# The norms' factors spread by two f32r passes instead of one f32 product

## The reference

```
for l in range(2):                                   # model A; B has the same frame
    x = x + 0.5 * swiglu(rmsnorm(x, ffn1_norm[l]), w_ffn1_in[l], w_ffn1_out[l])
    u = rmsnorm(x, mix_norm[l])
    c_q, c_kv, k_r, hq, hf, hi, hgate, mq, gates = split(u @ w_in[l])
    q = rmsnorm(c_q, q_lat_norm[l]) @ w_uq[l]         # the latents' norms, in A alone
    ckv = rmsnorm(c_kv, kv_lat_norm[l])
    mem_n = rmsnorm(mem, mem_norm[l])                 # the memory's norm, in A alone
    ...
    x = x + merged @ w_out[l]
    x = x + 0.5 * swiglu(rmsnorm(x, ffn2_norm[l]), w_ffn2_in[l], w_ffn2_out[l])
return rmsnorm(x, final_norm)

rmsnorm(x, g) = x * rsqrt(mean(x * x, over the width) + 1e-6) * g
```

## Time and profile before

| | us |
|---|---|
| median of 3 runs | 2376.81 |
| lowest and highest | 2376.17, 2376.86 |
| the profiled execution | 2377.26 |
| its span, from the first instruction to the last | 2375.5 |
| PE busy (99%) | 2356.3 |
| DVE busy (69%) | 1648.9 |
| ACT busy (53%) | 1253.1 |
| POOL busy (15%) | 363.4 |

### The profile page before, as it was taken

How to read it: one execution, slowest core, us unless ns; L and a number is a source line. 1 busy time by engine, 2 the same in 40 slices (tenths; PEclk the granted TensorE clock), 3 DMA queues, 4 the chain that set the end, 5 groups by cost and what they waited for, 6 DMA issues and landing times.

```text
span 2375.5 us, 50987 instructions
## 1 busy us (share of the span) xinstructions
PE 2356.3 (99%) x21836; PEld 2296.3 (97%) x21836; DVE 1648.9 (69%) x2292; ACT 1253.1 (53%) x1788; POOL 363.4 (15%) x313
## 2 busy tenths in 40 slices
PE   9999999999999999999999999999999999999998
PEld 8999999999999999999999999989999999989998
DVE  7775787966667657878666766776665766776764
ACT  6554656654445456565454454645554454645553
POOL 4012020300200210203003003431002002431001
PEclk9999999999999999999999999999999999999999
DMA  7555433455555544345555655413555555412553
GB/s 258 188 195 187 169 127 141 178 195 190 187 191 193 199 178 177 109 143 181 199 191 178 227 186 193 163 69 108 197 194 179 197 184 193 169 71 101 203 196 124
DMA packets 57680, 410.21 MB, mean 173 GB/s; under 512 B 6384, under 2 KB 6640, under 8 KB 8688
## 3 DMA queue, kind: packets, MB, share of 16 engines
q1 hardware_dynamic: 56592, 402.15, 47.2%
q10 hardware_dynamic: 864, 4.82, 0.5%
HBM read 405.89 MB, written 1.05 MB: 171 GB/s over the span
## 4 chain that ended last, share of the span: by engine, by line
PE 92%; DVE 4%; issue 2%; ACT 2%; DMA 0%; POOL 0%; SPq 0%; DVEq 0%; POOLq 0%; ACTq 0%
PE bank L301 91%; DVE area L314 1%; DVE sb_wlo L314 1%; ACT area L310 1%; PE bank L305 1%; DMA sb_raw<-stream 0%; ACT sb_whi L310 0%; POOL sb_x_ssq L314 0%; DVE area L325 0%; DVE area L342 0%; SPq L395 0%; DVE area L352 0%; DVE sb_x L325 0%; DVE area L320 0%; DVE sb_x L314 0%
## 5 line engine op out<-in xcount | busy, mean ns | idle before, releaser
L301 PE MATMUL bank<-area,sb_whi 128*128 128x256 f32 x11752 | 2040.3, 279 | 4.0 <-ACT area L310 2.5
L301 PEld LDWEIGHTS bank<-area,sb_whi 128*128 128x128 f32 x11752 | 1780.4, 188 | 15.3 <-ACT area L310 5.2
L301 PE MATMUL bank<-area,sb_wlo 128*128 128x256 f32 x5876 | 1619.6, 278 | 2.4 <-DVE sb_wlo L314 2.4
L310 ACT ACTIVATE sb_whi<-sb_raw 128x1024 fp32r<-128x1024 f32 x762 | 800.1, 1057 | 730.5 <-PE bank L301 726.9
L301 PEld LDWEIGHTS bank<-area,sb_wlo 128*128 128x128 f32 x5876 | 1100.3, 188 | 4.0 <-DVE sb_wlo L314 3.8
L314 DVE TENSOR_TENSOR sb_wlo<-sb_raw,sb_whi 128x1024 fp32r<-128x1024 f32 x762 | 957.6, 1265 | 167.4 <-ACT sb_whi L310 166.1
L314 DVE TENSOR_TENSOR area<-area,area 128x256 f32<-128x256 f32 (+6 forms) x504 | 258.9, 523 | 233.2 <-ACT area L310 231.5
L310 ACT ACTIVATE area<-area 128x256 fp32r<-128x256 f32 (+5 forms) x487 | 230.5, 482 | 66.2 <-DVE area L314 55.6
L314 DVE TENSOR_TENSOR area<-bank,sb_x_diag 128x512 f32<-128x512 f32 x244 | 166.8, 684 | 32.8 <-PE bank L301 19.3
L301 PE MATMUL bank<-area,area 64*64 64x64 f32 (+5 forms) x2864 | 151.0, 250 | 0.2
L301 PEld LDWEIGHTS bank<-area,area 64*64 64x64 f32 (+3 forms) x2864 | 128.7, 139 | 19.4 <-issue 4.9
(11 more groups left out here) (82 smaller groups left out, 722.9 us busy)
## 6 DMA issues: line engine op xcount, KB each, us to landing
sb_raw<-stream SPq DMA_DIRECT2D x379, 1024.0 KB, 4.8
sb_raw<-stream SPq DMA_DIRECT2D x4, 512.0 KB, 7.5
area<-lora ACTq DMA_DIRECT2D x2, 768.0 KB, 4.6
area<-c ACTq DMA_DIRECT2D x1, 1504.0 KB, 8.5
sb_x<-x SPq DMA_DIRECT2D x4, 256.0 KB, 5.4
area<-mem ACTq DMA_DIRECT2D x1, 1024.0 KB, 6.8
out<-sb_x SPq DMA_DIRECT2D x4, 256.0 KB, 2.9
area<-m ACTq DMA_DIRECT2D x1, 512.0 KB, 3.6
```

The lines of the kernel that those rows point to most:

```text
L301: return lambda e: e.matmul(out, lhsT, rhs, start=start, stop=stop, skip_group_check=True, tile_position=at)
L310: return lambda e: e.activation(out, a, f, **kw)
```

## The change

The diagonal tile is made twice: `high`, rounded to f32r as it is written, and `low`, the product again less `high`. `spread_parts` multiplies both by a matrix of ones in f32r and adds the results in PSUM. This replaces the float32 product in `norm_spread` (norms of x, of the memory, and both at the boundary) and in `latents_norm`. The final norm keeps the float32 product (`parts=False`). The ones in f32r are made once, by a copy on ACT in `constants_ready`, for which PE waits. The new tiles lie in memory of their own; `sc.diag` stays as the place of `sc.rs`.

```diff
@@ -698,11 +698,34 @@
     if at is None:
         sc.ssq, sc.diag, sc.sq = (sbuf(k, f"{name}_{n}", [128, T])[:, :] for n in ("ssq", "diag", "sq"))
         sc.ms, sc.tm = (sbuf(k, f"{name}_{n}", [128, 2])[:, :] for n in ("ms", "tm"))
+        sc.parts = [sbuf(k, f"{name}_{n}", [128, T], F32R)[:, :] for n in ("high", "low")]
     else:
         sc.ssq, sc.diag, sc.sq = (area(k, at + T * i, T) for i in range(3))
         sc.ms, sc.tm = area(k, at + 3 * T, 2), area(k, at + 3 * T + 8, 2)
+        sc.parts = [area(k, at + (4 + i) * T, T, dt=F32R) for i in range(2)]
     sc.rs = sc.diag
     return sc
+
+
+def diagonal_parts(k, parts, tm):
+    dve, ident = k.dve, const(k, "ident")
+    high, low = parts
+    for i in range(tm.shape[1]):
+        c, scale = slice(128 * i, 128 * i + 128), tm[:, i:i + 1]
+        n = dve.mark(tensor_scalar(high[:, c], ident, scale, ALU.mult))
+        dve.wait(dve, n)
+        n = dve.mark(scalar_tensor_tensor(low[:, c], ident, scale, high[:, c].bitcast(F32), ALU.mult, ALU.subtract))
+    return n
+
+
+def spread_parts(k, out, parts):
+
+    for i, part in enumerate(parts):
+        n = k.pe.mark(matmul(out, k.ones_r, part, start=i == 0, stop=i == 1))
+    return n
 
 
 def square(k, sc, j, x):
@@ -724,7 +747,7 @@
     return n
 
 
-def norm_sums(k, sc, b, more=None):
+def norm_sums(k, sc, b, more=None, parts=True):
 
 
     pe, dve, pool = k.pe, k.dve, k.pool
@@ -742,6 +765,9 @@
     pool.wait(dve, n)
     sc.tm_done = pool.mark(tensor_tensor(sc.tm, sc.ms, col(k, COL_HALFNEG).to_broadcast([128, 2]), ALU.pow))
     dve.wait(pool, sc.tm_done)
+    if parts:
+        sc.diag_done = diagonal_parts(k, sc.parts, sc.tm)
+        return
     for i in range(2):
         sc.diag_done = dve.mark(tensor_scalar(sc.diag[:, 128 * i:128 * i + 128], const(k, "ident"),
                                               sc.tm[:, i:i + 1], ALU.mult))
@@ -750,7 +776,7 @@
 def norm_spread(k, sc, b):
 
     k.pe.wait(k.dve, sc.diag_done)
-    n = k.pe.mark(matmul(b[:, T:2 * T], const(k, "ones"), sc.diag))
+    n = spread_parts(k, b[:, T:2 * T], sc.parts)
     k.act.wait(k.pe, n)
     sc.rs_done = k.act.mark(activation(sc.rs, b[:, T:2 * T], ACT.Copy))
 
@@ -833,7 +859,7 @@
 def final(k):
 
     pe, dve, b = k.pe, k.dve, k.bank[3]
-    norm_sums(k, k.sx, b, k.last.more)
+    norm_sums(k, k.sx, b, k.last.more, False)
     pe.wait(dve, k.sx.diag_done)
     n = pe.mark(matmul(b[:, T:2 * T], const(k, "ones"), k.sx.diag))
     dve.wait(k.act, k.x_done[NX - 1])
@@ -890,10 +916,9 @@
     pool.wait(dve, n)
     n = pool.mark(tensor_tensor(f.tm, f.ms, col(k, COL_HALFNEG).to_broadcast([128, 4]), ALU.pow))
     dve.wait(pool, n)
-    ident = const(k, "ident")
-    for diag, c in ((k.sx.diag, 2), (f.diag, 0)):
-        for i in range(2):
-            n = dve.mark(tensor_scalar(diag[:, 128 * i:128 * i + 128], ident, f.tm[:, c + i:c + i + 1], ALU.mult))
+    f.parts = [area(k, SPARE + (5 + i) * T, T, dt=F32R) for i in range(2)]
+    for parts, c in ((k.sx.parts, 2), (f.parts, 0)):
+        n = diagonal_parts(k, parts, f.tm[:, c:c + 2])
     k.sx.diag_done = f.diag_done = n
 
 
@@ -1218,7 +1243,8 @@
 
     m.lat, m.lsq = area(k, 0, 6, T), area(k, 6 * T, 5, T)
     m.lat_hi, m.lat_lo = area(k, 11 * T, 5, T, dt=F32R), area(k, 16 * T, 5, T, dt=F32R)
-    m.lat_diag = m.lat_rs = area(k, 21 * T, 512)
+    m.lat_rs = area(k, 21 * T, 512)
+    m.lat_parts = [area(k, at * T, 512, dt=F32R) for at in (21, 25)]
     m.k_rot = [area(k, (23 + i) * T, T) for i in range(2)]
     m.q_rot = [area(k, 6 * T + 512 * i, 2, T) for i in range(2)]
     m.gates = [area(k, T * i if i < 20 else 44 * T + T * (i - 20), 2, T) for i in range(0, 24, 2)]
@@ -1337,16 +1363,14 @@
     pool.wait(dve, n)
     n = pool.mark(tensor_tensor(m.lat_tm, m.lat_ms, col(k, COL_HALFNEG).to_broadcast([128, 4]), ALU.pow))
     dve.wait(pool, n)
-    for i in range(4):
-        m.lat_diag_done = dve.mark(tensor_scalar(m.lat_diag[:, 128 * i:128 * i + 128], const(k, "ident"),
-                                                 m.lat_tm[:, i:i + 1], ALU.mult))
+    m.lat_diag_done = diagonal_parts(k, m.lat_parts, m.lat_tm)
 
 
 def latents_norm(k, m, l):
     pe, act, dve = k.pe, k.act, k.dve
     b = k.bank[6]
     pe.wait(dve, m.lat_diag_done)
-    n = pe.mark(matmul(b[:, :], const(k, "ones"), m.lat_diag))
+    n = spread_parts(k, b[:, :], m.lat_parts)
     act.wait(pe, n)
     n = act.mark(activation(m.lat_rs, b[:, :], ACT.Copy))
     dve.wait(act, n)
@@ -2675,6 +2699,7 @@
         for q in (k.pe, k.act, k.dve, k.pool):
             q.wait(*k.constants)
         k.constants = None
+        k.pe.wait(k.act, k.act.mark(activation(k.ones_r, const(k, "ones"), ACT.Copy)))
 
 
 def store(k):
@@ -2697,6 +2722,7 @@
         k.bank = [k.psum[:, i, :] for i in range(8)]
         k.x, k.vecs, k.c1 = sbuf(k, "x", [128, NX, T]), sbuf(k, "vecs", [128, NV]), sbuf(k, "c1", [128, NC1])
         k.sx, k.scratch = scales(k, "x"), sbuf(k, "scratch", [128, 2])[:, :]
+        k.ones_r = sbuf(k, "ones_r", [128, 128], F32R)[:, :]
         k.placed = 0
         low = place(k, nc.sbuf_usable_end // 32 * 32)
         ctx.enter_context(nc.sbuf_tensor("placed", [128, (nc.sbuf_usable_end - low) // 32 * 8], F32, side="right"))
```

## The result

The kernel after takes 2381.1 us in the median of 16 runs (2378.45 to 2383.35), the kernel before beside it 2376.84 (16 runs, 2375.48 to 2380.15). The medians differ by 4.3 us or 0.18%; the ratio, which goes by the means, is 1.0015 with an interval of 1.0008 to 1.0021, that is 1.9 to 5.0 us slower. That is inside the forecast range and within 0.2%, but the size was forecast as +1.7. The profiled execution took 2383.35 us with a span of 2381.5; against the profiled execution of before that is +6.1 us. It is the slowest of the 16, 2.25 us above their median, so its trace shows where the time goes, but more of it than the median has.

The account below looks back on a forecast made before the run. PE bounds the kernel, busy 2356.3 of 2375.5 us. Terms -1.76, +0.87, +0.96, +0.03, -0.06, +1.40 and +0.25 sum to +1.7 us; on the median 2376.81 that is 2378.5 us, range 2374.3 to 2383.0.

Parts of the forecast that it names:

- B0f1: Both boundary norms: the spreads wait for the last of four tiles on DVE, 1.27 us late, net +0.96 us.
- The price of a spread: On PE, two f32r passes replace a float32 product of 256 columns, giving back 0.195 us; nine covered spreads give -1.76 us.
- DVE's chain: Product, wait and remainder per tile on DVE make the diagonal 0.77 us later for two tiles, 1.54 for four.
- the wait is free: Rival: on DVE the remainder starts 0.20 us after its product; -0.3 us in all, 2376.5 us, chance 0.15.
- everything is covered: Rival: the later diagonals delay nobody on PE; -3.5 us, 2373.3 us, chance 0.14.
- the rival at 0.215: Rival: an f32r pass with ones as weights costs 0.215 us on PE instead of 0.118; +4.4 us, 2381.2, chance 0.04.
- B0f2 and B1f2: Two short spreads whose diagonals come 0.15 and 0.06 us late for PE: net +0.03 and -0.06 us.
- A1mix: Latents' norm there: PE's `values` waits for its bank's evacuation, delayed 1.67 us on DVE; +1.40 us.
- PE's own wait for the copy is over long before its sums.: At the start, PE's wait for the ones costs nothing; only the copy's 0.25 us on ACT counts.
- Latents, A0mix: Latents' norm there: the same delayed bank evacuation ahead of PE's `values`, 1.6 us looser; +0.25 us.
- the rival of the DVE backlog: Rival: later `split_lo` work on DVE makes PE wait; 14.9 us if PE paid it all, 2388.2 us, chance 0.09.
- After these places PE runs without idle time again and gives nothing back.: Beyond the listed spreads and latents, PE's remaining work neither gains nor loses time: 0 us.

Follow-up runs that it names:

- e3: The changed kernel with the ones made by two DVE instructions at the very start and no copy on ACT: 2377.74 us, ratio 0.9998 to the kernel before.
- e5: e3 with the rounded products of all tiles ahead of all remainders on DVE: 2375.42 us against 2376.79 for the kernel before, ratio 0.9993.
- e4: The changed kernel with the latents' norms spread by the float32 product again: 2376.2 us, ratio 0.9994 to the kernel before.
- e1: The kernel before plus only the ones' copy on ACT and PE's wait for it ahead of the first sums: 2380.16 us against 2377.45, ratio 1.0009.
- e7: The kernel before with the ones made at the start and only the two latents' norms changed: 2379.23 us, ratio 1.001.
- e8: e7 with one more low part of the weights made on DVE during POOL's power, ahead of the latents' diagonals: 2381.39 us, ratio 1.0018 to the kernel before.
- e12: The kernel before, unchanged, timed and profiled once more: 2377.05 us against 2377.2, ratio 0.9999.
- e2: The changed kernel with PE's wait for the ones moved from the first sums to the first spread: 2378.34 us, ratio 1.0002 to the kernel before.

## Why the prediction was right, and where it wasn't

The time lies in the range and the sign is the forecast one, but both are partly luck. The reason given was that the gain of 0.195 us a spread is smaller than what the longer diagonals cost at the few places with no slack. The places themselves bear it out (-1.74 at the covered ones, +4.0 at the latents and B0f1), but the stretches give 1.7 back, and the whole change without PE's wait for the ones (e3) is level with before: +0.3 us, interval -2.6 to +1.7. So the slowdown in the medians is for the most part that wait, for which the sum had nothing beyond the copy's 0.25. The upper end of the range, 2383, came from a remainder of 0.59 us; the remainder took 0.35. And the rival whose time, 2381.2, is nearest to the measured 2381.1 has a mechanism that the trace refutes. These steps held:
- The price of a spread: nine covered ones give -1.74 (forecast -1.76); none lost its cover.
- DVE's chain: the remainder took 0.35 us (0.345), the next product started 0.27 after it (0.265), and the wait cost 0.035 (0.034); two tiles last 1.26 us (1.245). The rivals "the wait is free" and "everything is covered" fall: they need a chain of about 1.0 us, or no idle PE at 1312. The drain rule that I had weighed against the rows (the Trainium skill, "VectorE: DVE Perf Modes", section "The DRAIN you can't avoid") says, of eight tensor_copies in a row, that a semaphore after each costs nothing extra. This case disagrees for its small instructions: with the waits in between, four instructions take 1.26 us, with both products first 0.99 (e5).
- The f32r pass with the ones as weights costs 0.12, as in the gemms: the rival at 0.215 falls.
- B0f1 (+1.05 for +0.96), B0f2 and B1f2 (-0.01, -0.05 for +0.03, -0.06), and A1mix with its mechanism, the bank (+1.45 for +1.40).

Three steps failed.

**"PE's own wait for the copy is over long before its sums."** This was the large one. I gave the copy a place on ACT's queue by the DMA issue at 21.79 and the split at 21.84: the copy stands in the program ahead of the three DMA issues, so it seemed to stand ahead of that split. But the issues are handed out by ACT's sequencer ahead of splits that stand before them in the program; in after, all three issues (22.87 to 24.02) come earlier than the copy at 25.53, which the program has in front of them. So the copy stood behind three splits that follow each other at 0.95 us, not ahead of them, and the wait that `constants_ready` puts in front of PE's sums made a gap of 4.5 us (1.2 and 1.5 in the two profiles of before) and a stretch at half clock, against 0.25 us in my sum. In the trace the start is +4.71 for +0.87; in the medians the wait is worth 1.4 to 4.0 us (e4, e1, after against e3). The prediction asked what a copy on ACT delays on ACT, and took the wait on PE for settled without finding the end of what lay ahead of it.

**Latents, A0mix: +0.25, measured +1.50.** I asked only for the bank. `values` also waits, ahead of its first pass, for the low part of its first piece, and DVE makes that behind the very evacuation whose delay I had counted. In before it ended shortly ahead of its use: the evacuation starts at 269.28, the first of the two parts behind it ended at 271.14, and the spread frees PE at 271.56. With 1.67 us more on DVE it had only 0.42 to give: 1.67 - 0.42 + 0.10 for the restart + 0.08 = +1.43. That is the rival of the DVE backlog, true at this one place and nowhere else. (Its price of 14.9 us counts 13 norms of two tiles. There are 12: DVE has 36 instructions more, 12 x 2 and 3 x 4. It should be 14.1.) Its argument against itself, that each part is made two pieces ahead, doesn't hold where a unit's evacuation and the splits lie behind one long chain. e4 and e7 show the size, the profile of after and e8 the releaser.

**"After these places PE runs without idle time again and gives nothing back."** It gave back 1.5 us at four stretches and 0.2 at two more, where the float32 spread had kept the spacing of the passes at 0.118 instead of 0.1138. I had looked at the spread and its neighbours only; no row of before alone could show this, since every spread in it is float32.

The second and third cancel roughly (+1.25, -1.7), so that the sum missed by about the ones' wait. With e1's 2.7 in place of the 0.25 it is 1.7 + 1.25 - 1.7 + 2.45 = 3.7, where 4.3 was measured with an interval from 1.9 to 5.0.

## What to carry to other kernels

A constant made once still has a place on a queue and a waiter. Find the instruction of its own kind (not a DMA issue) that stands ahead of it, take its end in the trace, and compare it with the time at which the waiter wants to go on; or make the constant at the start, where all engines are idle. When an engine gets longer work ahead of others, follow everything behind it on its queue up to its first use, and look at each thing that the waiting engine needs, not only at the one that came last before. And a gain in one engine's work that needs longer work on another is best taken only where the slack exceeds the delay: here that, with the ones made at the start, turned +4.3 us into -3.5.

## What the runs showed of the hardware

- DMA issues on ACT's queue appear in the trace, and happen, ahead of ACTIVATEs that the program has before them (22.87, 23.29 and 24.02 ahead of 25.53 in after; by 25.5 us their queue has moved 0.37 MB).
- A float32 product of 256 columns can cost more than its own 0.43 us: behind four of the fourteen short spreads, some 84 passes of the steady gemm that follows come 0.118 us apart instead of 0.1138, 0.37 us in all, beginning 60 to 70 passes later. At these four places all fourteen profiles show it, each on the side of its spread's form; at most of the others there is nothing of the kind, and the reason is open.
- An idle gap of PE of 4.3 to 4.5 us at the start was followed by 6.8 us at half clock (e1, after), a gap of 1.5 with two shorter ones behind it by 3.4 (e12, e2), and a gap of 1.0 or 1.2 with one wait of 0.16 behind it by none (e3, before).
- POOL's power of 128x4 elements took 1.94 us where DVE had just begun a TENSOR_TENSOR with two inputs in SBUF, 1.04 without (e8, e7). The Trainium skill has the rule ("SBUF — State Buffer", section "Who interferes with whom"): a DVE instruction with two SBUF inputs and a GpSimd one that reads SBUF exclude each other, and the later one waits. The rows agree: DVE runs to 266.47, and POOL ends 0.89 after that.
- The weights of one early split arrive at times that differ by some 0.8 us between executions (in the two profiles of before the next split starts at 21.84 without a wait and at 22.60 after 1.11 us of waiting for its DMA). The second of them is 2.16 us later by pass 160, with the clock at half after the longer gap.
